# Up- and down-projection of each feed-forward half in one stage instead of two, with waits for single tiles between them

## The reference, cut to what matters

```python
def swiglu(h, w_gate_up, w_down):
    gate, up = jnp.split(h @ w_gate_up, 2, axis=-1)
    return (jax.nn.silu(gate) * up) @ w_down

fx = rms_norm(x, g_ffn[i]) * (1.0 + sc2) + sh2
x = x + ga2 * swiglu(fx, w_gate_up[i], w_down[i])
if update_ctx:
    fc = rms_norm(ctx, g_ffn[i]) * (1.0 + csc2) + csh2
    ctx = ctx + cga2 * swiglu(fc, w_gate_up[i], w_down[i])
```

## Time and profile before

| | |
|---|---|
| median of 3 runs | 3449.82 us |
| runs | 3446.94 to 3450.13 us |
| profiled execution, its own time | 3449.35 us |
| its span, first to last instruction | 3447.4 us |
| mean granted TensorE clock | 0.976 |
| busy share: PE, PEld, DVE, ACT, POOL | 94%, 74%, 44%, 34%, 43% |
| DMA, mean over the span | 82 GB/s |

### The profile page before, as it was taken

One profiled execution on the slowest core, in us unless ns is written; L12 is line 12 of the kernel. 1 busy time (PEld: TensorE's weight loads), 2 busy tenths in 40 slices (PEclk: granted clock), 3 DMA queues, 4 the chain that ended last, 5 costly groups with the idle time before them and its releaser, 6 DMA issues. The chain is left out here.

```text
span 3447.4 us, 52077 instructions
## 1 busy us (share of the span) xinstructions
PE 3234.4 (94%) x21116; PEld 2538.9 (74%) x21116; DVE 1518.6 (44%) x2402; ACT 1171.6 (34%) x1914; POOL 1485.0 (43%) x820
## 2 busy tenths in 40 slices
PE   8899999999798999989998989999999988999999
PEld 6784776788577747867876756888888875678787
DVE  6643274899676332848996136300000022620000
ACT  5224433422352334343224535322122133532121
POOL 4422553454343225534542257344234434745454
PEclk9999999999899999999999999999999999999999
DMA  3011122555120111325542200121221111022322
GB/s 131 3 34 45 60 99 67 203 194 199 58 78 3 39 55 50 110 86 189 196 176 87 90 25 20 50 68 50 68 68 62 62 59 49 8 86 91 97 94 90
DMA packets 77469, 284.19 MB, mean 82 GB/s; under 512 B 8592, under 2 KB 8592, under 8 KB 76720
## 3 DMA queue, kind: packets, MB, share of 16 engines
q1 hardware_dynamic: 77232, 280.87, 24.3%
HBM read 278.74 MB, written 2.10 MB: 81 GB/s over the span
## 5 line engine op out<-in xcount | busy, mean ns | idle before, releaser
L131 POOL TENSOR_TENSOR lows<-ring,highs 128x1024 fp32r<-128x1024 f32 x376 | 938.1, 2496 | 1625.3 <-ACT highs L123 1608.5
L155 PE MATMUL ps<-x_high,highs 128*128 128x512 f32 x1936 | 772.3, 399 | 35.1 <-ACT highs L123 16.3
L158 PE MATMUL ps<-x_low,highs 128*128 128x512 f32 x1936 | 760.1, 393 | 0.0
L123 ACT ACTIVATE highs<-ring 128x1024 fp32r<-128x1024 f32 x376 | 397.2, 1057 | 770.9 <-PE ps L155 391.0
L155 PEld LDWEIGHTS ps<-x_high,highs 128*128 128x128 f32 x1936 | 366.3, 189 | 125.3 <-issue 30.7
L158 PEld LDWEIGHTS ps<-x_low,highs 128*128 128x128 f32 x1936 | 366.5, 189 | 78.3 <-issue 3.5
L2680 DVE TENSOR_TENSOR hidden_scratch<-ps,hidden_scratch 128x512 f32<-128x512 f32 x44 | 30.4, 692 | 545.8 <-PE ps L2040 541.8
L669 PE MATMUL ps<-x_high,lows 128*128 128x512 f32 x1040 | 256.9, 389 | 0.0
L669 PEld LDWEIGHTS ps<-x_high,lows 128*128 128x128 f32 x1040 | 195.3, 188 | 40.4
L2591 DVE SCALAR_TENSOR_TENSOR BR<-ps,mod,BR 128x512 f32<-128x512 f32 x72 | 47.4, 661 | 387.8 <-PE ps L167 387.8
L163 PE MATMUL ps<-hidden_parts,highs 128*128 128x512 f32 (+1 forms) x528 | 191.7, 363 | 12.0 <-PEq L2614 12.0
(11 more groups left out here) (434 smaller groups left out, 5881.3 us busy)
## 6 DMA issues: line engine op xcount, KB each, us to landing
ring<-in_w SPq DMA_DIRECT2D x414, 512.0 KB, 3.5
merging<-in_ada SPq DMA_DIRECT2D x48, 512.0 KB, 3.5
BR<-in_ada SPq DMA_DIRECT2D x48, 512.0 KB, 3.5
X<-in_xT SPq DMA_DIRECT2D x4, 512.0 KB, 6.8
X<-in_memT SPq DMA_DIRECT2D x2, 1024.0 KB, 5.1
merging<-in_cond SPq DMA_DIRECT2D x4, 512.0 KB, 4.8
out<-BR SPq DMA_DIRECT2D x8, 256.0 KB, 4.5
cst<-in_cst SPq DMA_DIRECT2D x1, 1408.0 KB, 8.0
```

The lines of the kernel that those rows point to most:

```text
L123: nc.scalar.activation(self.high(n), self.chunk(n), ACT.Copy).then_inc(self.hi_made, 1)
L131: nc.gpsimd.tensor_tensor(self.low(n), self.chunk(n), self.high(n).bitcast(F32), ALU.subtract).then_inc(self.lo_made, 1)
L155: mm = nc.tensor.matmul(ps, high, xhigh, start=start, stop=False)
L158: nc.tensor.matmul(ps, high, xlow, start=False, stop=False)
```

## The change

The function `project` becomes a class `Project` whose methods `sync`, `tensor`, `scalar`, `pool` and `vector` hold what each engine did, without a Block of their own. The out-projection wraps them in a Block, as before. In the feed-forward each engine runs its part of the down-projection directly behind its part of the up-projection, inside the one Block; the barrier between the two, one call of `stage()` and one clearing of a semaphore pool per half are gone. PE waits, before each contraction step of the first output tile, for that hidden tile's low part (`lows`), and before each of the first four outputs for the last reader of its bank (`freed`). The banks of the down-projection are turned by two (`turn`), so that its first two outputs go to those of the last hidden tile but one; the sums of squares and the norm that reads them in layer 1 are turned as well. The down-projection's semaphores get names of their own in the same pool.

```diff
-            def __init__(self, S, which, shift, sts, slots, inverse):
+            def __init__(self, S, which, shift, sts, slots, inverse, turn=0):
+                self.turn = turn
...
-                nc.scalar.activation(self.inverse[s["name"]], PS[:, s["bank"], 0:s["n"]], ACT.Ln, scale=1.0 / D, bias=eps).then_inc(self.S("log" + s["name"]), 1)
+                nc.scalar.activation(self.inverse[s["name"]], PS[:, s["bank"] + self.turn, 0:s["n"]], ACT.Ln, scale=1.0 / D, bias=eps).then_inc(self.S("log" + s["name"]), 1)
...
-        def project(first, kt, rhs, gate, split=(), squares=None, store=False):
-            S, other = stage()
-            with nc.Block() as block:
-                @block.sync
-                def _(sp):
-                    stream.send(sp, first + RING)
-                    clear(sp, other)
-                    stream.send(sp, first + chunks + RING - 1)
...
+        class Project:
+            def bank(self, s, m):
+                return PS[:, s["bank"] + (m + self.turn) % 4, 0:s["n"]]
+            def sync(self, sp):
+                S = self.S
+                stream.send(sp, self.first + self.kt + RING - 1)
...
+            def tensor(self, pe):
+                S, first, kt, squares = self.S, self.first, self.kt, self.squares
+                for m in range(8):
+                    if m >= 4:
+                        for s in full:
+                            pe.wait_ge(S("added" + s["name"]), m - 3)
+                    elif self.freed is not None:
+                        self.freed(pe, m)
...
+                            for k in ks:
+                                b = (m * kt + k) % 8
+                                if m == 0:
+                                    pe.wait_ge(self.lows("low" + s["name"]), k + 1)
+                                mm = three(nc, self.bank(s, m), tile_of(stream.high(n), b), tile_of(stream.low(n), b),
+                                           high[:, k, :], low[:, k, :], k == 0, k == kt - 1, mark(n, i == 0 and b == 0))
...
         for part in range(2):
             n0 = at[f"up{part}"]
             S, other = stage()
+            below = lambda name, S=S: S("down_" + name)
+
+            def hidden_freed(pe, m, S=S):
+                for s in full:
+                    pe.wait_ge(S("act" + s["name"]), FH - 1 if m < 2 else FH)
+
+            down = Project(below, at[f"down{part}"], FH, FFN, GA2, S, (), {"x": tiles_of(scratch, 0, 2), "c": tiles_of(scratch, 2, 2, CTX)} if part and update else None,
+                           part and not update, 2, hidden_freed)
...
                     stream.send(sp, n0 + 2 * FH + RING - 1)
+                    down.sync(sp)
...
                             gemm(pe, n0 + 2 * t + j, [(PS[:, s["bank"] + 2 * (t % 2) + j, 0:s["n"]], s["h"], s["l"], S(("gate", "up")[j] + s["name"])) for s in full])
+                    down.tensor(pe)
...
                     high(FH - 1)
+                    down.scalar(act)
...
                     low(FH - 1)
+                    down.pool(pool)
...
+                    down.vector(dve)
...
-            project(at[f"down{part}"], FH, FFN, GA2, (), {"x": tiles_of(scratch, 0, 2), "c": tiles_of(scratch, 2, 2, CTX)} if part and update else None, part and not update)
```

More of the change, by code:

```diff
@@ L2160, in second @@
         norm = Norm(S, 0, SH1, streams if layer else streams[:1], {"x": tiles_of(work, 0, 4), "c": tiles_of(work, 4, 4, CTX)},
-                    {"x": tiles_of(work, 8 if layer == 0 else 6), "c": tiles_of(work, 7)[:, 0:CTX]})
+                    {"x": tiles_of(work, 8 if layer == 0 else 6), "c": tiles_of(work, 7)[:, 0:CTX]}, 2 if layer else 0)
         last = Last(S, work)
@@ L2493, in second @@
                   [Y[:, a * T:(a + 3) * T] for a in (9, 12)], XT(29), opening=output_lows)
-        def project(first, kt, rhs, gate, split=(), squares=None, store=False):
-            S, other = stage()
-            chunks = kt
-            def behind(m):
-                return min(first + kt * (m + 1) // 8 + 2, first + chunks + 1)
-            with nc.Block() as block:
-                @block.sync
-                def _(sp):
-                    stream.send(sp, first + RING)
-                    clear(sp, other)
-                    stream.send(sp, first + chunks + RING - 1)
[L2511 to L2518, removed]
-                    for m in range(8):
[L2520 to L2538, removed]
-                    if squares is not None:
[L2540 to L2545, removed]
-                        for s in full:
[L2547 to L2588, removed]
-                        for s in full:
-                            dve.wait_ge(S("product" + s["name"]), m + 1)
-                            nc.vector.scalar_tensor_tensor(out=s["src"][:, m, :], in0=PS[:, s["bank"] + m % 4, 0:s["n"]], scalar=mod[:, gate + m, s["k"]:s["k"] + 1],
-                                                           in1=s["src"][:, m, :], op0=ALU.mult, op1=ALU.add).then_inc(S("added" + s["name"]), 1)
@@ L2600, in second, with _ @@
             with nc.sbuf_tensor(f"output_squares{layer}", [P, 3 * T], F32) as sq:
-                project(at["out"], 8, {"x": (MH, ML), "c": (MHc, MLc)}, GA1, split, {"x": tiles_of(sq, 0, 2), "c": tiles_of(sq, 2, 2, CTX)})
+                S, other = stage()
+                out = Project(S, at["out"], 8, {"x": (MH, ML), "c": (MHc, MLc)}, GA1, S, split, {"x": tiles_of(sq, 0, 2), "c": tiles_of(sq, 2, 2, CTX)})
+                with nc.Block() as block:
+                    @block.sync
+                    def _(sp):
+                        stream.send(sp, at["out"] + RING)
+                        clear(sp, other)
+                        out.sync(sp)
+                    @block.tensor
+                    def _(pe):
+                        out.tensor(pe)
+                    @block.scalar
+                    def _(act):
+                        out.scalar(act)
+                    @block.gpsimd
+                    def _(pool):
+                        out.pool(pool)
+                    @block.vector
+                    def _(dve):
+                        out.vector(dve)
         room.close()
```

66 lines of the change are left out of this document (added).

## The result

The changed kernel takes 3431.85 us (median of 5 runs, 3425.11 to 3433.18); the kernel before, beside it, 3446.94 (5 runs, 3446.04 to 3450.13). The ratio is 0.995, with a 95% interval of 0.9935 to 0.9965: small, but clear of no change. The forecast was 3430.8.

A forecast was written before the change was run, and what follows sets the result against it. PE was taken to bound the kernel, busy 3234.4 of 3447.4 us. Hole 12.7 plus clock 6.5 minus 0.2 at the seam gave 19.0 us, so 3430.8 from the median 3449.82; range 3426 to 3438.

The forecast's parts named there:

- The hole: PE's idle time between up- and down-projection closes: 3.30 us in layer 1, 3.03 in layer 0, twice each, 12.7 us.
- The clock: Behind each of four seams the first 24 matmuls lose 1.63 us to low clock; 6.5 us saved if it stays up.
- The order at the seam: In layer 1 the second down chunk is split 0.2 us before PE wants it; 0.1 us charged at two seams.
- Transfers: Third and later down chunks are issued earlier, no longer behind the barrier; cost and gain nothing.
- Added waits: 90 more PE waits in the down-projections, for low parts and freed banks; taken at nothing.
- the rival of 51 ns each: Each of the 90 added waits holds PE for 51 ns, 4.6 us, hence 3435.4; chance 0.04.
- Turned banks: Down-projection begins at bank 2, layer 1's first-norm sums of squares land in bank 2 or 6; cost nothing.
- the rival of the remaining stop: PE still stops at each seam for DVE's last product, four times 1.0 us, 3434.8; chance 0.04.
- clock falls elsewhere: Rival: the clock falls anyway, at later idle places or still at the seams; all 6.5 us lost, 3437.3; chance 0.12.
- The split did not fall behind over the whole down-projection: Rival: ACT's and POOL's split runs late, PE stops at each of layer 1's 22 chunks; slower, 3462; chance 0.02.

The follow-up runs named there:

- e3: The changed kernel, but PE waits before its first down-projection step for all eleven low parts of both streams; 3446.9 us, 0.9992 of the kernel before.
- e8: The kernel before with nine filler matmuls on PE in the hole behind the up-projection, barrier kept; 3443.82 us, 0.9986 of the kernel before.
- e2: The kernel before with twelve filler matmuls on PE in the hole behind the up-projection, barrier kept; 3446.97 us, 0.9989 of the kernel before.
- e7: The changed kernel with two more POOL operations ahead of the second down chunk's split; 3438.19 us, 0.9969 of the kernel before.
- e5: The changed kernel with a low-part wait before every contraction step of every output tile, not the first alone; 3432.32 us, 0.9952 of the kernel before.
- e6: The changed kernel without the turn of the banks, in down-projection and norm; 3432.14 us, 0.9949 of the kernel before.
- e1: The changed kernel run again with no edit; 3434.16 us, 0.9954 of the kernel before.
- e11: The changed kernel run a third time with no edit; 3431.51 us, 0.9951 of the kernel before.
- e9: The changed kernel with three more POOL operations ahead of the second down chunk's split; 3439.7 us, 0.9971 of the kernel before.
- e4: The changed kernel with both halves of a layer's feed-forward in one Block; 3429.08 us, 0.9936 of the kernel before.
- e10: Both halves of a layer's feed-forward in one Block, run again beside the changed kernel; 3429.23 us, 0.9944 of the kernel before.

## Why the prediction was right

- **The hole.** The sum had 12.7 us. By the distance of the last up group and the first down matmul it is 3.98 - 0.95 = 3.03 in each half of layer 0 and 5.11 - 1.82 = 3.29 in each of layer 1, so 12.6. e3 shows what made it: the wait for the last low part, with 0.2 us of barrier on top. The prediction had left that split unpriced.
- **The clock.** 6.5 us were forecast; the 24 matmuls went from 7.23 to 5.62 us, 6.4 together, and e8 gives 6.0 by itself, with the hole in place. Its condition, that PE's idle time brings the fall, is shown from both sides: filled, no fall (e2, e8); open again without a barrier, four falls (e3). This holds for the seams; the last section shows places where it does not.
- **The order at the seam.** PE was to want the second chunk 0.2 us behind its split. It was 0.27, and no stop came; the 0.2 charged for two seams was not spent. e7 shows that the margin is real and as thin as that.
- **Transfers.** Taken at nothing, and so it is: PE has no idle time at all in the four stretches.
- **Added waits.** Taken at nothing against the rival of 51 ns each; e5 adds 462 more and finds nothing, and most of them are no instructions of their own. The figure of 50 to 100 ns from the Trainium skill (Advanced Engine Details and Errata, Network/Comms) may hold for the reading of a semaphore, but e5's stretches show none of it on PE's path.
- **Turned banks.** I costed the turn itself at nothing, which holds. What it saves I named only in the rival of the remaining stop, at 4.0 us; e6 measured 3.9.
- **The sum.** 19.0 us forecast, 19.0 in the stretches. The medians show 15 to 17. That the time itself, 3431.85, came within 1.1 us of the 3430.8 is in part luck: the forecast was counted from a median of 3449.82, and the kernel before took 3446.94 beside the changed one. The range had kept room for clock falls elsewhere, and that was needed: the same kernel's rest moved by 7.7 us between three profiles.
- **The rivals.** The clock did not fall at the seams, and low clock elsewhere did not grow (0.12): outside the seam stretches the trace has it for 145 us in the changed kernel, 154 before. The split did not fall behind over the whole down-projection (0.02): in e7 even a delay of 2.55 us made one stop per product in layer 1, and no second one.

Where the rest of the span moves can be read from the three profiles of the changed kernel. Outside the seams the clock was at 1.2 GHz for 145 us in the first, 154 in e1 and 131 in e11, in the order of their rests (3114.8, 3118.6, 3110.9 us). The largest single step from the first profile to e1 is 2.5 us in layer 1's attention, where the clock was low for 13.2 us instead of 3.4; the largest to e11 is 1.6 us near 940, in the first block, with 10.0 us of low clock instead of 16.5. So the largest steps are clock falls elsewhere. Some of the movement does not come from the clock: the first 25 us of the program differ by up to 1.2 us at full clock. Nor does time at 1.2 GHz always cost: the kernel before has a rest of 3114.0 with 154 us of it, and ahead of layer 1's input product it cost nothing, as shown above. Why the clock falls in one execution and not in the next stays open.

## What to carry to other kernels

A barrier between two stages can hide a wait for one last tile that the next stage doesn't need at first. Look for what the first instruction behind it really reads; let it start on that, with the last tile as the last step of its sum, and give it a bank that was left a tile ago. Price the hole and the clock behind it apart, since fillers on PE recovered the second here with the first left open, and check which engine's chain becomes the next to be late, as POOL's here by 0.27 us.

## What the runs showed of the hardware

PE's recorded idle time ahead of a matmul, and whether a fall of the clock to 1.2 GHz followed, can be set side by side. First the seams. After 0.3 to 1.1 us (e2, e6 and e8) none did; after 2.07 in both places of e7 none; after 2.66 to 3.29 one did in all ten places (four each in the kernel before and in e3, two in e9). It cost 1.6 us, once 2.8.

Elsewhere in the second block the length of the idle time alone doesn't decide. In both layers PE is idle for 1.88 us ahead of the ten matmuls of line 2100. Near 2220, in layer 0, a fall followed within 1 us in all 13 profiles; near 2790, in layer 1, within 1.3 us in five of them (the kernel before, e3, e4, e6, e10). Layer 1's attention has two idle times of 3.3 us near 2920. Behind the first of them the clock fell within 1.3 us in 11 profiles, and stayed up for 5 us in two (the changed kernel's first and e11). The table by windows from PE's start behind that idle time to the end of PE's next idle time, in the changed kernel

```profile
2916.22:2921.11 4.89, 1.56 (x9) 1.00 0.01 3
```

and in the same kernel's run e1:

```profile
2918.61:2924.44 5.83, 2.51 (x8) 0.54 0.01 3
```

In e1 another fall had ended 3 us ahead of that start, in the first profile none. The kernel before had none ahead of it either, and there the clock fell all the same.

After 2.42, ahead of layer 1's out-projection, it fell in ten profiles, among them the kernel before, and stayed up in three (e3, e6, e8), with the same instructions and the same idle time. The table by windows for 6 us behind that start, in the kernel before

```profile
3011.45:3017.45 6.00, 6.00 (x19) 0.72 0.53 143
```

and in e6:

```profile
3003.74:3009.74 6.00, 6.00 (x26) 1.00 0.49 145
```

I had not expected to see this so plainly: the same hole costs a fall in one execution and none in another. So these traces give no single length above which the clock falls: 1.88 us was followed by a fall at one place every time, and 3.31 at another sometimes not. What happens in one execution and not in the next is a source of spread in the runs that no edit of the kernel explains, and a reason to read effects of a few microseconds from the stretch where they arise.
